# A step list of the sliding-window mixer reordered: unit 2's scores ahead of unit 1's value product, side steps up to two places later

## The chip, the cores and the metric

The kernel runs on one core of one Trainium2 chip. The metric is the time of one execution on the device in microseconds (us), lower is better. The engines are TensorE (PE in the rows, its weight loads PEld), VectorE (DVE), ScalarE (ACT), GpSimd (POOL) and SyncE (SP), which issues all the loads of weights.

## What is computed

Two models of two layers each run one after the other on a sequence of 256 positions with 1024 features. The change touches one sublayer only, the sliding-window attention with sinks in the last layer of the second model:

```python
def swa_sink_attention(h, wqkv, bqkv, qnorm, knorm, sinks, wo, bo):
    qkv = h @ wqkv + bqkv
    q, k, v = jnp.split(qkv, [ATTN_HEADS * HD, (ATTN_HEADS + KVH) * HD], axis=-1)
    q = rms_norm_2(q.reshape(bsz, T, KVH, G, HD), qnorm)
    k = rms_norm_2(k.reshape(bsz, T, KVH, HD), knorm)
    ...
    s = jnp.where(mask[None, :, None, None], s, -jnp.inf)      # scores, less a slope times distance
    p = jax.nn.softmax(jnp.concatenate([s, sink], axis=-1), axis=-1)[..., :-1]
    o = jnp.einsum('bnhgqk,bnkhd->bnqhgd', p.astype(h.dtype), vv)
    return o.reshape(bsz, T, ATTN_HEADS * HD) @ wo + bo
```

There are 16 query heads of 64 features and 4 heads of keys and values; the window is 128 positions. Ahead of this sublayer lie the whole first model and the second model's first layer and a feed-forward part; behind it a cross-attention to a memory (scores, softmax, value product, output projection) and a last feed-forward part.

## The kernel before, in words

Each engine has a program of its own, written out by hand, and the engines meet by semaphores only: an engine does its steps strictly in the order of its program and stops at the first one whose inputs are not there. Every dense product is made of three TensorE products of rounded halves (`hi` and `lo` of the weights, `thi` and `tlo` of the activations); ScalarE (L595) and VectorE (L607) split the weights that SyncE loads.

The sublayer is called `swa`. Its 16 heads and 256 positions are cut in six **units**, numbered 0 to 5. Units 0 to 2 have the first eight heads, units 3 to 5 the last eight. Units 0 and 3 are the first 128 positions with eight heads; the others are the last 128 positions with four heads and 256 keys. Each unit u has five **steps** (u, p):

- (u, 0) scores, on TensorE: two products that bring in the mask (L2869), then the score products (L2879), into banks 0 and 1 for an even unit and 2 and 3 for an odd one. With `lean` set it waits until unit u-2 has been copied out of the same banks.
- (u, 1) maxima, on VectorE: L996, L1006, L1010, L1011.
- (u, 2) exponentials, on ScalarE: L1066 for each head, L1069 for the sink.
- (u, 3) transposes of the probabilities: TensorE L963; VectorE sums the sink and inverts (L1018, L1021) and copies one half out (L1029); ScalarE copies the other half (L1073).
- (u, 4) value product: TensorE L978, and VectorE scales it into the output (L1047).

Beside these run **side steps**, one at each `None` of the list `SWA_PLAN`. They are written as generators on each engine, and the n-th `None` is the n-th piece of work of all of them. The ones that matter here:

- side step 4 (the last query quarter): TensorE makes the last quarter of the product with `wq2`, which gives the queries of heads 8 to 15 (six products, L645 to L647); VectorE takes both halves of the result out with the bias (L3008 twice; the second of them needs this quarter).
- side step 5 (squares and means): ScalarE squares these queries (L2962 twice), VectorE reduces and scales the sums (L3035, L3038 twice), and GpSimd raises them to a power (L841, twice).
- side step 6 (scaling): VectorE multiplies the queries by the result (L3045 twice).
- side step 7 (turning): TensorE transposes them (L728), ScalarE and VectorE write the rounded halves (L740, L757). Unit 3's scores need these.
- side step 8 transposes the outputs of units 0 to 2 (L728 again, ahead of unit 4's scores) and the following ones multiply them by the output weights (L645 to L647).

`placed` turns the list into the order of the unit steps and the places of the side steps, and `mixed` runs both in this order on TensorE, VectorE and ScalarE alike:

```python
    def mixed(main, side, places):
        at = 0
        for place in places:
            while at < place:
                next(main)
                at += 1
            next(side)
        run(side)
        run(main)
```

Of the kernel before, what the change touches and what calls it, by code (L numbers as in the profile page):

```python
# [456 lines left out]
def placed(plan):  # L457

    steps, places = [], []
    for x in plan:  # L460
        if x is None:
            places.append(len(steps))
        else:
            steps.append(x)
    return steps, places
# [32 lines left out]
class Kernel:  # L498
# [2360 lines left out]
    def swa_units(self):  # L2859
# [24 lines left out]
        for half in range(2):  # L2884
            for tt, h0, n in ((0, 8 * half, 8), (1, 8 * half, 4), (1, 8 * half + 4, 4)):
# [8 lines left out]

    SWA = {"k": (0, 4, 160), "q0": (512, 8, 96), "q1": (1024, 8, 0)}

    SWA_PLAN = [(0, 0), (0, 1), (1, 0), (0, 2), (1, 1), None, None, (0, 3), (1, 2), None, (0, 4), (1, 3), None, (1, 4),
# [3 lines left out]
    SWA_ORDER, SWA_BESIDE = placed(SWA_PLAN)  # L2901

# [847 lines left out]
```

How the kernel before makes its waits and increments, by code:

```python
def arms(e, c, flag, known, yes, no, stage):  # L378
    start, seen, chunks, splits = Counter(c.n), dict(c.seen), c.chunks, c.splits
    if c.dry:
        yes()
        after = Counter(c.n)
        c.n, c.chunks, c.splits = Counter(start), chunks, splits
        no()
        c.K.at["pad", stage, c.name] = Mark(c.name, max(after[c.name], c.n[c.name]))
        c.n[c.name] = c.K.at["pad", stage, c.name].value
    else:
        total = c.K.at["pad", stage, c.name].value
        for w in c.need(known):
            e.wait_ge(*w)
        seen = dict(c.seen)
        taken = e.value_load(flag, min_val=0, max_val=1)
        with e.If(taken == 1):
            yes()
            if c.n[c.name] < total:
                for w in c.need(c.last):
                    e.wait_ge(*w)
                e.nop().then_inc(*c.tick(by=total - c.n[c.name]))
        c.n, c.chunks, c.splits, c.seen = Counter(start), chunks, splits, dict(seen)
        with e.Else():
            no()
            if c.n[c.name] < total:
                for w in c.need(c.last):
                    e.wait_ge(*w)
                e.nop().then_inc(*c.tick(by=total - c.n[c.name]))
        c.seen = dict(seen)
    c.K.at["joined", stage, c.name] = c.last
# [167 lines left out]
    def load(self, s, c, i):  # L576
# [3 lines left out]
            if i >= NS:  # L580
                for w in c.need(("hi", i - NS, p), ("lo", i - NS, p)):
                    s.wait_ge(*w)
            b = (2 * i + p) % (2 * NS)
```

## Time and profile before

| what | value |
|---|---|
| time, median of 3 runs | 2207.06 us (2205.02 to 2209.64) |
| the profiled execution | 2209.44 us, span 2207.6 us |
| granted TensorE clock, mean of the span | 0.975 of full speed |
| TensorE matmuls busy | 95% of the span |
| VectorE, ScalarE, GpSimd busy | 70%, 56%, 2% |
| share of the 16 DMA engines used | 57.9% |

The span is what the trace covers; the profiled execution took 1.84 us more than it. The stretch that the change reorders lies between 1882 and 1908 us of the span. "Granted clock" is the share of TensorE's full clock of 2.4 GHz: 1.00 is 2.4 GHz and 0.50 is 1.2 GHz.

### The profile page before, as it was taken

The numbers are of one execution on the slowest core, as the hardware profiler recorded it, in microseconds if no ns is written. First come the engines' busy times: TensorE is split into PE (matmuls) and PEld (weight loads), VectorE is DVE, ScalarE is ACT, GpSimd is POOL, SyncE is SP. The second block draws the span as 40 slices with busy tenths as digits, with TensorE's granted clock in tenths as the row PEclk, the third lists the DMA queues.
The fourth block names the chain that finished last, engine by engine and source line by source line (L and its number), as shares of the span: only waits on it lengthen the run. The fifth ranks groups of instructions, "written<-read, shape, count | busy, mean of one in ns | idle before, by whom it ended". The sixth has DMA issues, their size and how long they took to land.

```text
span 2207.6 us, 32321 instructions
## 1 busy us (share of the span) xinstructions
PE 2095.2 (95%) x12148; PEld 1830.9 (83%) x12148; DVE 1545.2 (70%) x2158; ACT 1232.6 (56%) x1973; POOL 51.8 (2%) x64
## 2 busy tenths in 40 slices
PE   7988999989889999999999999999999999899999
PEld 5777888867677888878998987799999997779998
DVE  6568999986668999986555666566566566655655
ACT  4545777755546777755444564554444445454443
POOL 0000000000000000010000000000000001000000
PEclk9998999999989999999999999999999999899999
DMA  6233999973227999965556534255555555134553
GB/s 245 84 110 130 378 360 356 364 296 110 96 82 275 366 374 361 358 233 164 189 178 192 166 122 136 100 171 186 191 173 189 192 177 188 58 115 142 184 193 112
DMA packets 124214, 446.80 MB, mean 202 GB/s; under 512 B 14320, under 2 KB 15472, under 8 KB 123120
## 3 DMA queue, kind: packets, MB, share of 16 engines
q1 hardware_dynamic: 124048, 444.61, 57.9%
q8 instruction: 101, 1.65, 0.3%
q14 instruction: 65, 0.53, 0.1%
HBM read 443.51 MB, written 1.05 MB: 201 GB/s over the span
## 4 chain that ended last, share of the span: by engine, by line
PE 49%; DVE 3%; ACT 2%; issue 1%; DMA 0%; POOL 0%; DVEq 0%; SPq 0%; ACTq 0%
PE bank L686 8%; PE bank L688 8%; PE bank L687 8%; PE bank L1106 4%; PE bank L1105 4%; PE bank L1107 4%; PE bank L645 4%; PE bank L647 3%; PE bank L646 3%; PE bank L2725 1%; DVE lo L607 1%; PE bank L2707 1%; PE bank L978 1%; ACT hi L595 0%; DMA scr<-in_alibi 0%
## 5 line engine op out<-in xcount | busy, mean ns | idle before, releaser
L607 DVE TENSOR_TENSOR lo<-stage,hi 128x1024 fp32r<-128x1024 f32 (+1 forms) x834 | 971.6, 1207 | 233.5 <-ACT hi L595 206.6
L595 ACT ACTIVATE hi<-stage 128x1024 fp32r<-128x1024 f32 (+1 forms) x834 | 831.1, 1040 | 224.8 <-PE bank L647 83.6
L686 PE MATMUL bank<-thi,hi 128*128 128x256 f32 x1504 | 427.5, 284 | 5.1 <-DVE tlo L762 3.1
L687 PE MATMUL bank<-tlo,hi 128*128 128x256 f32 x1504 | 426.3, 283 | 0.0
L688 PE MATMUL bank<-thi,lo 128*128 128x256 f32 x1504 | 426.2, 283 | 0.0
L686 PEld LDWEIGHTS bank<-thi,hi 128*128 128x128 f32 x1504 | 289.2, 192 | 8.0 <-issue 6.5
L687 PEld LDWEIGHTS bank<-tlo,hi 128*128 128x128 f32 x1504 | 289.3, 192 | 1.4
L688 PEld LDWEIGHTS bank<-thi,lo 128*128 128x128 f32 x1504 | 289.2, 192 | 0.0
L645 PE MATMUL bank<-hi,thi 128*128 128x512 f32 (+3 forms) x648 | 253.9, 392 | 19.9 <-DVE tlo L762 6.9
L647 PE MATMUL bank<-hi,tlo 128*128 128x512 f32 (+3 forms) x648 | 248.0, 383 | 0.0
L646 PE MATMUL bank<-lo,thi 128*128 128x512 f32 (+3 forms) x648 | 247.9, 382 | 0.0
L2367 PE MATMUL bank<-hi,scr_r 128*128 128x512 f32 x512 | 206.5, 403 | 7.3 <-DVE scr_r L2497 5.8
L2369 PE MATMUL bank<-hi,scr_r 128*128 128x512 f32 x512 | 201.8, 394 | 0.0
L2368 PE MATMUL bank<-lo,scr_r 128*128 128x512 f32 x512 | 201.4, 393 | 0.0
L645 PEld LDWEIGHTS bank<-hi,thi 128*128 128x128 f32 x648 | 123.6, 191 | 47.1 <-issue 12.8
L647 PEld LDWEIGHTS bank<-hi,tlo 128*128 128x128 f32 x648 | 123.2, 190 | 23.4
L1131 ACT ACTIVATE scr<-scr 128x256 f32<-128x256 f32 x66 | 27.6, 418 | 204.2 <-DVE scr L1166 204.2
L646 PEld LDWEIGHTS bank<-lo,thi 128*128 128x128 f32 x648 | 123.6, 191 | 21.5 <-issue 0.4
L1105 PE MATMUL bank<-hi,ahi 128*128 128x512 f32 x352 | 137.5, 391 | 0.0
L1106 PE MATMUL bank<-lo,ahi 128*128 128x512 f32 x352 | 137.4, 390 | 0.0
L1107 PE MATMUL bank<-hi,alo 128*128 128x512 f32 x352 | 137.0, 389 | 0.0
L2367 PEld LDWEIGHTS bank<-hi,scr_r 128*128 128x128 f32 x512 | 97.1, 190 | 27.3 <-ACT hi L595 8.3
(395 smaller groups left out, 2709.8 us busy)
## 6 DMA issues: line engine op xcount, KB each, us to landing
stage<-in_exp SPq DMA_DIRECT2D x384, 512.0 KB, 5.3
stage<-in_ffn SPq DMA_DIRECT2D x264, 512.0 KB, 4.2
stage<-in_wi_a SPq DMA_DIRECT2D x16, 512.0 KB, 6.4
stage<-in_wi_b SPq DMA_DIRECT2D x16, 512.0 KB, 4.6
stage<-in_mem_wkv SPq DMA_DIRECT2D x16, 512.0 KB, 5.1
stage<-in_xwq SPq DMA_DIRECT2D x16, 512.0 KB, 4.2
stage<-in_xwo SPq DMA_DIRECT2D x16, 512.0 KB, 4.3
stage<-in_ssd_xbc SPq DMA_DIRECT2D x12, 512.0 KB, 3.8
```

The source lines that it names most:

```text
L595: a.activation(self.hi[i % NR][:, x:y], self.stage[(2 * i + p) % (2 * NS)][:, :y - x], ACT.Copy).then_inc(*c.tick(("hi", i, p), sem="hi"))
L607: v.tensor_tensor(self.lo[i % NR][:, x:y], self.stage[(2 * i + p) % (2 * NS)][:, :y - x], self.hi[i % NR][:, x:y].bitcast(F32), ALU.subtra ...
L645: t.matmul(out, thi[:, xs], hi[:, ws], start=(k0 + j == 0), stop=False)
L646: t.matmul(out, thi[:, xs], lo[:, ws], start=False, stop=False)
L647: m = t.matmul(out, tlo[:, xs], hi[:, ws], start=False, stop=(k0 + j == kt - 1))
L686: t.matmul(out, hi[:, ws], self.thi[:, xs], start=(k == 0), stop=False)
L687: t.matmul(out, hi[:, ws], self.tlo[:, xs], start=False, stop=False)
L688: m = t.matmul(out, lo[:, ws], self.thi[:, xs], start=False, stop=(k == 7))
L1105: t.matmul(out, self.ahi[:, xs], hi[:, ws], start=(f + j == 0), stop=False)
L1106: t.matmul(out, self.ahi[:, xs], lo[:, ws], start=False, stop=False)
L1107: m = t.matmul(out, self.alo[:, xs], hi[:, ws], start=False, stop=(f + j == nf - 1))
L2367: t.matmul(out, R["ghi"][:, xs], hi[:, ws], start=(k == 0), stop=False)
```

## The change

One table is edited: in `SWA_PLAN`, (2, 0) moves ahead of (1, 4), and of the side steps 4, 5, 6 and 7 each comes behind one or two unit steps that it stood ahead of. No instruction is added or removed, and the list has as many entries as before.

```diff
-    SWA_PLAN = [(0, 0), (0, 1), (1, 0), (0, 2), (1, 1), None, None, (0, 3), (1, 2), None, (0, 4), (1, 3), None, (1, 4),
-                (2, 0), None, (2, 1), None, (2, 2), (2, 3), None, (2, 4),
+    SWA_PLAN = [(0, 0), (0, 1), (1, 0), (0, 2), (1, 1), None, None, (0, 3), (1, 2), None, (0, 4), (1, 3), (2, 0), (1, 4),
+                None, (2, 1), (2, 2), None, (2, 3), None, (2, 4), None,
                 (3, 0), (3, 1), None, (4, 0), (3, 2), (4, 1), None, None, (3, 3), (4, 2), None, (3, 4), None,
```

**TensorE, from the transposes of unit 1 to the turning of the queries.** Before: L963 are transposes of probabilities, L645 to L647 the last query quarter, L978 a value product, L2869 and L2879 scores, L728 the turning.

```order
L963 MATMUL bank<-const_sb,scr 128x128 x8
L645 MATMUL bank<-hi,thi 128x512
...
L647 MATMUL bank<-hi,tlo 128x512
L978 MATMUL bank<-scr 128x64 x8
L2869 MATMUL bank<-scr_r,maskr 128x512 x2
L2879 MATMUL bank<-scr_r 128x256 x4
...
L963 MATMUL bank<-const_sb,scr 128x128 x8
L728 MATMUL bank<-const_sb,scr 128x128 x8
L978 MATMUL bank<-scr 128x64 x8
L2869 MATMUL bank<-scr_r,maskr 128x512 x2
```

After, the same place:

```order
L963 MATMUL bank<-const_sb,scr 128x128 x8
L2869 MATMUL bank<-scr_r,maskr 128x512 x2
L2879 MATMUL bank<-scr_r 128x256 x4
...
L978 MATMUL bank<-scr 128x64 x8
L645 MATMUL bank<-hi,thi 128x512
...
L647 MATMUL bank<-hi,tlo 128x512
L963 MATMUL bank<-const_sb,scr 128x128 x8
L978 MATMUL bank<-scr 128x64 x8
L728 MATMUL bank<-const_sb,scr 128x128 x8
L2869 MATMUL bank<-scr_r,maskr 128x512 x2
```

Unit 2's scores now stand ahead of unit 1's value product, the query quarter comes behind both, and the turning comes behind unit 2's value product instead of ahead of it.

**VectorE, the same stretch,** one piece of the difference. L3008 takes the queries out, L1047 scales a value product, L3035 and L3038 are the means, L996 to L1011 unit 2's maxima.

```order
 L1029 COPY scr<-bank 128x512
+L1047 TENSOR_TENSOR gb_<-bank,st 128x2x2x64
 L3008 SCALAR_TENSOR_TENSOR scr<-bank,st,rows 128x512 x2
-L1047 TENSOR_TENSOR gb_<-bank,st 128x2x2x64
+L996 TENSOR_REDUCE st<-bank 128x2 x2
+L1006 SCALAR_TENSOR_TENSOR st<-st,rows 128x4
+L1010 TENSOR_TENSOR st<-rows,st 128x4
+L1011 TENSOR_SCALAR st<-st 128x4
 L3035 TENSOR_REDUCE st<-scr 128x8
 L3038 TENSOR_SCALAR st<-st 128x8
```

The maxima of unit 2 now come ahead of the means but behind the taking out of the queries. Further down, the means stand ahead of unit 2's copy L1029, and the scaling L3045 behind it.

**ScalarE, from unit 1's copy on.** Before, the squares L2962 stand ahead of unit 2's exponentials L1066:

```order
L1073 ACTIVATE scr<-bank 128x512
L2962 ACTIVATE scr<-scr 128x512 x2
L1066 ACTIVATE scr,st<-bank,st 128x256 x4
L1069 ACTIVATE st<-st 128x4
L1073 ACTIVATE scr<-bank 128x512
```

After, they stand behind them:

```order
L1073 ACTIVATE scr<-bank 128x512
L1066 ACTIVATE scr,st<-bank,st 128x256 x4
L1069 ACTIVATE st<-st 128x4
L2962 ACTIVATE scr<-scr 128x512 x2
L1073 ACTIVATE scr<-bank 128x512
```

The squares moved behind the exponentials, and what follows from them moved with them. GpSimd's and SyncE's programs are the same as before.

## Rows read from the trace of the kernel before

**Rows 1.** The page: engine totals, and the chain that ended last.

```profile
PE 2095.2 (95%) x12148; PEld 1830.9 (83%) x12148; DVE 1545.2 (70%) x2158; ACT 1232.6 (56%) x1973; POOL 51.8 (2%) x64
...
PE 49%; DVE 3%; ACT 2%; issue 1%; DMA 0%; POOL 0%; DVEq 0%; SPq 0%; ACTq 0%
```

**Rows 2.** Windows: from:to, length, busy by engine, then granted clock, DMA share, GB/s.

```profile
1878.00:1888.00 10.00, 8.94 (x70) 7.58 (x68) 6.72 (x15) 4.00 (x13) 0.43 (x1) 1.00 0.32 107
...
1891.00:1908.00 17.00, 16.04 (x92) 14.60 (x92) 6.35 (x14) 5.94 (x22) 0.00 (x0) 0.50 0.00 0
1908.00:1918.00 10.00, 10.00 (x66) 8.16 (x64) 7.29 (x14) 5.35 (x19) 0.00 (x0) 1.00 0.35 107
```

**Rows 3.** Timeline, TensorE: start, length, instruction, count, idle time before it.

```profile
1882.06 1.04 PE L963 MATMUL bank<-const_sb,scr 128*128 128x128 f32 x8
...
1882.86 0.48 PE L645 MATMUL bank<-hi,thi 128*128 128x512 f32 x1
...
1884.33 1.89 PE L978 MATMUL bank<-scr 128*128 128x64 f32 x16
...
1886.04 0.72 PE L2869 MATMUL bank<-scr_r,maskr 128*128 128x512 f32 x2
...
1891.96 1.97 PE L963 MATMUL bank<-const_sb,scr 128*128 128x128 f32 x8 [4.07 <-ACT scr L1066]
...
1893.73 1.91 PE L728 MATMUL bank<-const_sb,scr 128*128 128x128 f32 x8
...
1895.43 3.52 PE L978 MATMUL bank<-scr 128*128 128x64 f32 x16
...
1898.71 1.20 PE L2869 MATMUL bank<-scr_r,maskr 128*128 128x512 f32 x2
...
1903.44 1.97 PE L728 MATMUL bank<-const_sb,gb_ 128*128 128x128 f32 x8
...
1908.17 0.50 PE L645 MATMUL bank<-hi,thi 128*128 128x512 f32 x1
```

**Rows 4.** Timeline, the other engines in the same stretch.

```profile
1882.26 0.69 DVE L1047 TENSOR_TENSOR gb_<-bank,st 128x512 f32<-128x512 f32 x1 [2.15 <-PE bank L978]
...
1883.75 1.53 DVE L3008 SCALAR_TENSOR_TENSOR scr<-bank,st,rows 128x512 f32<-128x512 f32 x2
...
1885.32 0.63 ACT L2962 ACTIVATE scr<-scr 128x512 f32<-128x512 f32 x1 [0.16 <-DVE scr L3008]
...
1887.39 0.68 DVE L3035 TENSOR_REDUCE st<-scr 128x8 f32<-128x512 f32 x1
...
1887.57 3.23 POOL L841 TENSOR_TENSOR st<-st,const_sb 128x8 f32<-128x8 f32 x2 [22.92 <-DVE st L3038]
...
1888.19 1.28 DVE L996 TENSOR_REDUCE st<-bank 128x2 f32<-128x512 f32 x2
...
1889.98 0.47 ACT L1066 ACTIVATE scr<-bank,st 128x256 f32<-128x256 f32 x1 [4.03 <-DVE st L1011]
...
1890.83 0.69 DVE L3045 TENSOR_TENSOR scr<-scr,st 128x512 f32<-128x512 f32 x1 [0.30 <-POOL st L841]
...
1891.79 0.21 ACT L1069 ACTIVATE st<-st 128x4 f32<-128x4 f32 x1
...
1893.97 0.69 DVE L1029 COPY scr<-bank 128x512 f32<-128x512 f32 x1 [1.56 <-PE bank L963]
...
1896.31 0.69 DVE L757 TENSOR_TENSOR scr_r<-bank,scr_r 128x512 fp32r<-128x512 f32 x1 [0.16 <-ACT scr_r L740]
```

**Rows 5.** Timeline, TensorE: the scores of unit 5, at the full clock.

```profile
1916.63 0.63 PE L2869 MATMUL bank<-scr_r,maskr 128*128 128x512 f32 x2
...
1918.33 1.09 PE L963 MATMUL bank<-const_sb,scr 128*128 128x128 f32 x8
```

**Rows 6.** Windows: the softmax of both cross-attentions of the second model.

```profile
1418.00:1424.00 6.00, 4.81 (x29) 4.39 (x28) 3.04 (x6) 2.27 (x8) 0.00 (x0) 0.72 0.00 0
...
1977.00:1987.00 10.00, 7.12 (x35) 6.32 (x34) 5.59 (x11) 4.34 (x14) 0.00 (x0) 0.66 0.01 2
```

## The prediction

> **What bounds the kernel now.** I read the page first. TensorE is busy 95% of the span and has 49% of the chain that ended last; no other engine has more than 3% of it [rows 1]. So an edit is worth what it does to TensorE's own stream: time in which TensorE waits, and the clock at which it works. Next I read the windows over the stretch that the list orders. Three stages are to be seen [rows 2]: up to 1888 TensorE works at the full clock; from 1891 to 1908 it is busy 16.04 of 17.00 us, but at a granted clock of 0.50; from 1908 on it is busy without a break at 1.00. Then the timeline. Ahead of unit 2's transposes at 1891.96 TensorE is idle for 4.07 us, waiting for ScalarE's exponentials [rows 3]. These began at 1889.98, when VectorE had the maxima ready, whose reduction began at 1888.19 [rows 4]. In front of that reduction VectorE's last piece of the means began at 1887.39 and took 0.68 us [rows 4]: VectorE, not TensorE, is late there. Behind the wait TensorE runs transposes, turning, value product, scores (1891.96, 1893.73, 1895.43, 1898.71) back to back [rows 3], at half the clock.
>
> So two things can be won or lost here: the idle time ahead of unit 2's transposes, and any new idle time on the way to unit 3's scores, which began at 1898.71.
>
> **The change, part by part.** All instructions stay. I replay the order with the durations of the rows; nothing moves before 1882.06.
>
> *Unit 2's scores earlier.* Unit 1's transposes take 0.80 us (1882.06 to 1882.86) [rows 3]. The scores need unit 0 out of their banks: VectorE's L1047 ends at 1882.26 + 0.69 = 1882.95 [rows 4]. They begin at about 1883.05 instead of 1886.04. At the full clock they take 1916.63 to 1918.33 = 1.70 us [rows 5], so they end at 1884.75. Unit 1's value product, 1.71 us (1884.33 to 1886.04) [rows 3], ends at 1886.46. The query quarter, 1.47 us (1882.86 to 1884.33) [rows 3], ends at about 1887.9, where TensorE was done before too. So far this is the same work in another order and costs nothing.
>
> *Unit 2's maxima.* By TensorE's account alone they could begin 3 us earlier. But on VectorE they now stand behind L3008 twice, and the second L3008 needs the query quarter, which now ends last. The pair took 1.53 us (0.75 each) [rows 4]. The quarter's result lands about 0.25 us behind its last issue (an estimate: it was issued until 1884.33, and the pair, begun at 1883.75, started its second half at about 1884.5 without a wait). So the second L3008 runs from 1888.15 to 1888.9, and the maxima begin at 1888.95 instead of 1888.19 [rows 4]: **0.76 us later**. What was taken off VectorE's path (the means, two times 0.68 and a short one each) is more than replaced by the wait for the quarter. The exponentials follow at the old distance (1889.98 - 1888.19 = 1.79), so at 1890.74, and the transposes at 1892.72. TensorE's idle time ahead of them grows from 4.07 to about 4.8 us.
>
> *Squares, means, power, scaling.* ScalarE now does both squares (0.63 us each [rows 4]) behind the exponentials, which end at 1891.79 + 0.21 + 0.76 = 1892.76. The squares end at 1893.45 and 1894.1. VectorE's means follow each (0.68 and a short operation of 0.17): done at 1894.4 and 1895.35. GpSimd needs 3.23 us for its two [rows 4]: 1894.5 to about 1897.75. Before, all this was hidden: it ran while TensorE waited for unit 2's exponentials anyway, and the second scaling began at 1890.83 [rows 4]. That cover is gone. Two things are now late:
>
> - unit 2's copy L1029 stands behind the means on VectorE. Sum, inverse (about 0.45 together) and the copy's 0.69 us [rows 4] end at 1896.55. Unit 2's value product waits for it and begins at 1896.65. The transposes end at 1894.7, so this is a **new wait of about 1.95 us** on TensorE;
> - the second scaling begins at 1897.8 and ends at 1898.5. At the slow clock that lies under the value product, which takes 3.3 us (1895.43 to 1898.71) [rows 3] and ends at 1899.95. Nothing is lost there.
>
> *Turning behind the value product.* Before, the turning's way through ScalarE and VectorE (1893.73 to 1896.31 + 0.69 = 1897.0, so 3.3 us) [rows 3, 4] lay beside the value product, and TensorE had no gap. Now nothing stands between the turning and unit 3's scores, which need its last half. From 1899.95 the turning takes TensorE about 1.8 us, and its results are there at 1903.3: a **second new wait of about 1.55 us**. Unit 3's scores begin at 1903.35 instead of 1898.71.
>
> Sum: 1903.35 - 1898.71 = **+4.64 us**. Made another way: 0.76 later transposes, 1.95 and 1.55 us of new waits, and about 0.4 for the latency of the transposes and the turning, which are no longer covered. Behind that point the order is the old one and TensorE goes on back to back; the chain behind it lies on TensorE, so the shift reaches the end whole. No load waits on it: in the slow stretch the DMA share is 0.00 [rows 2].
>
> *The clock.* Before, the granted clock fell to 0.50 during the idle stretch (it is 0.50 over 1891 to 1908) and stayed there although TensorE was busy 16.04 of 17.00 us, with transposes, a value product of 64 columns and score products of 64 rows [rows 2, 3]. It came back at 1908, with the mask and score products of unit 4, just ahead of dense products. In the changed kernel the idle time is longer, so I expect the fall too, and the same kinds of work behind it, now with two more gaps. So I take the return at the same place in the work. The bounds: a return at unit 3's scores saves half of what lies between 1898.71 and 1908.17, 9.46 / 2 = 4.7 us, at the most [rows 3]; a return only in the dense products behind 1908.17 costs an estimated 1 to 2.8 us (the twelve products there, at twice their 0.24 us each, as the six of a quarter take 1.47 us [rows 3]).
>
> The Trainium skill ("TensorE: Matmul & The Clock Gate", Part 1) says that an idle TensorE is put at 1.2 GHz, and that a busy one soon gets 2.4 GHz back. The fall agrees with rows 2; the return doesn't, since 16 busy microseconds did not bring it. By that rule the clock would be back early in unit 3's scores, the second rival below.
>
> **Rivals.**
>
> 1. *The stated one* (late maxima, two new waits, clock as before): +4.6 us, 2211.7. Chance 0.50.
> 2. *The clock comes back with unit 3's scores or the transposes behind them.* For it: TensorE would have been busy for some microseconds by then. Against it: 16.04 busy us at 0.50 [rows 2]. It gives back some 1 to 3 us: +1.6 to +3.6, 2208.7 to 2210.7. Chance 0.17.
> 3. *Slow for longer.* The two new gaps put off the return into the dense products, or the slow part in the softmax of the following cross-attention lasts longer. For it: that part has a clock of 0.66 over 10 us, and the like part one layer earlier 0.72 over 6 [rows 6], so 3.4 us lost against 1.7, with the same work: such parts move by about 1.7 us. +6 to +7.5, 2213 to 2214.5. Chance 0.18.
> 4. *Not slower: the clock doesn't fall, or is back before unit 2's value product.* The place is the idle stretch at 1888. The earlier scores shift TensorE's work in it, and if the clock stays at 1.00, then the value product ends at 1896.65 + 1.71 = 1898.4, the turning begins at 1898.6 when the scaling is done and is through in about 2.5 us (3.3 less the half of its 1.8 on TensorE), unit 3's scores begin at 1901.1, and the 9.46 us behind that become 4.7 to 5.3: 1905.8 to 1906.4 against 1908.17, so -2.4 to -1.8 us, 2205. It decides if the wait of 4.8 us stays under whatever makes the clock fall; 4.07 us did not [rows 3], so against it speaks every row there is. Chance 0.10.
> 5. *The change does what its order suggests:* unit 2's maxima gain from the earlier scores since VectorE gets past L3008 sooner than I reckon, and the copy slips in before the means are due. If the second L3008 ran 0.8 us sooner, the first 0.76 us are gone and the rest stays: +3.9. With both squares and power quicker still, nothing under +2.5: 2209.6 to 2211. Chance 0.05.
>
> **How the numbers follow.** The profiled execution took 2209.44 us, span 2207.6 and 1.84 around it; the median of the three runs is 2207.06. The sum of +4.6 against the profiled execution gives 2214.1, against the median 2211.7. I give the latter, since the profiled one was at the upper end of the runs. Its own range is 2210 to 2213.5. The whole range is 2207 to 2214.5: it leaves out rival 4 and a tail above rival 3. A measurement of this kernel can tell about 0.2% (4.4 us) from no change, so the forecast lies just above that bound, and the chances are near even. Slower by over 0.2%: somewhat more than half of case 1 (0.32) and all of case 3 (0.18), 0.50. Within 0.2%: the rest of case 1 (0.18), cases 2 and 5 (0.22), and most of case 4 (0.06), 0.46. Faster by over 0.2%: 0.04, where rival 4 also loses the slow part of the following cross-attention.
>
> **What the profile of the changed kernel would show.** L996 for unit 2 begins at about 1889 behind the second L3008, which itself waited for L647. TensorE idle 4.8 us ahead of L963 at 1892.7, about 1.9 us ahead of L978 (released by VectorE's L1029), about 1.5 us ahead of L2869 (released by L757). L2869 of unit 3 at about 1903.3. Clock 0.50 from 1891 until about 1911 to 1915. I am wrong if L978 does not wait for L1029, if the clock in 1893 to 1903 is 1.00, or if unit 3's scores begin before 1901.

## The result, and the profile after

The changed kernel takes 2213.7 us (median of 8 runs, 2211.28 to 2216.45), the kernel before, timed beside it, 2205.69 us. The ratio is 1.0033, interval 1.0023 to 1.0043: slower by 7.3 us, between 5 and 9.5 (the two medians differ by 8.0). The prediction was 2211.7 us in a range of 2207 to 2214.5, on a shift of +4.6. Four of the executions timed in the experiments took between 2519 and 7261 us and are left out of every ratio.

The page hardly moves; it is shown so that nobody looks there for 7 us.

```profile
PE 2095.8 (95%) x12148; PEld 1829.5 (83%) x12148; DVE 1546.2 (70%) x2158; ACT 1231.6 (56%) x1973; POOL 51.8 (2%) x64
```

TensorE's timeline in the changed kernel, against [rows 3]:

```profile
1880.38 1.05 PE L963 MATMUL bank<-const_sb,scr 128*128 128x128 f32 x8
...
1881.32 0.73 PE L2869 MATMUL bank<-scr_r,maskr 128*128 128x512 f32 x2
...
1884.94 0.48 PE L645 MATMUL bank<-hi,thi 128*128 128x512 f32 x1
...
1891.07 1.97 PE L963 MATMUL bank<-const_sb,scr 128*128 128x128 f32 x8 [4.48 <-ACT scr L1066]
...
1894.34 3.65 PE L978 MATMUL bank<-scr 128*128 128x64 f32 x16 [1.31 <-DVE scr L1029]
...
1897.78 1.91 PE L728 MATMUL bank<-const_sb,scr 128*128 128x128 f32 x8
...
1901.20 1.19 PE L2869 MATMUL bank<-scr_r,maskr 128*128 128x512 f32 x2 [1.50 <-DVE scr_r L757]
...
1910.11 0.50 PE L645 MATMUL bank<-hi,thi 128*128 128x512 f32 x1
```

And the other engines, against [rows 4]:

```profile
1887.29 1.28 DVE L996 TENSOR_REDUCE st<-bank 128x2 f32<-128x512 f32 x2
...
1889.08 0.47 ACT L1066 ACTIVATE scr<-bank,st 128x256 f32<-128x256 f32 x1 [7.46 <-DVE st L1011]
...
1890.98 1.16 ACT L2962 ACTIVATE scr<-scr 128x512 f32<-128x512 f32 x2
...
1891.66 0.69 DVE L3035 TENSOR_REDUCE st<-scr 128x8 f32<-128x512 f32 x1 [2.62 <-ACT scr L2962]
...
1892.63 3.23 POOL L841 TENSOR_TENSOR st<-st,const_sb 128x8 f32<-128x8 f32 x2 [30.05 <-DVE st L3038]
...
1893.54 0.66 DVE L1029 COPY scr<-bank 128x512 f32<-128x512 f32 x1
...
1895.90 0.69 DVE L3045 TENSOR_TENSOR scr<-scr,st 128x512 f32<-128x512 f32 x1 [0.91 <-POOL st L841]
```

The starts must be read from a common point, since executions reach this stretch at different times. Over all fourteen traces read here unit 1's transposes begin between 1876.07 and 1888.40 us, though the programs ahead of them are the same: 12 us of spread that has nothing to do with the change. Counted from unit 1's transposes, unit 2's begin at 10.69 us (before 9.90) and unit 3's scores at 20.82 (before 16.65). Both new waits are there, each with the releaser that was named, 1.31 us by the copy L1029 and 1.50 us by L757.

Windows of the changed kernel: the clock is at half (1.2 GHz) for 20.5 us.

```profile
1880.38:1888.80 8.42, 6.20 (x50) 4.94 (x49) 4.73 (x11) 0.60 (x1) 0.00 (x0) 1.00 0.05 19
1888.80:1909.30 20.50, 15.42 (x82) 13.27 (x84) 8.86 (x21) 6.83 (x21) 3.23 (x2) 0.50 0.00 0
1909.30:1914.00 4.70, 4.70 (x35) 4.02 (x34) 3.22 (x7) 4.42 (x16) 0.00 (x0) 1.00 0.00 0
```

From here on "the stretch" is the time from the start of unit 1's transposes to the first product of the output weights (L645 behind unit 4's scores). In the two traces it is 1908.17 - 1882.06 = 26.11 us before and 1910.11 - 1880.38 = 29.73 after: +3.62 us, half of what the medians say.

### The profile page after: what moved, and what is told of

It is laid out like the page before. It is cut to its first block, busy times and chain, and to the rows that moved or that the text cites. A ratio compares the mean times of both kernels' runs of the same rounds, so it can differ in the third digit from the quotient of the medians.

```text
span 2209.4 us, 32321 instructions
## 1 busy us (share of the span) xinstructions
PE 2095.8 (95%) x12148; PEld 1829.5 (83%) x12148; DVE 1546.2 (70%) x2158; ACT 1231.6 (56%) x1973; POOL 51.8 (2%) x64
## 4 chain that ended last, share of the span: by engine, by line
PE 49%; DVE 3%; ACT 2%; issue 1%; DMA 0%; POOL 0%; DVEq 0%; SPq 0%; ACTq 0%
PE bank L686 8%; PE bank L687 8%; PE bank L688 8%; PE bank L1106 4%; PE bank L1105 4%; PE bank L1107 4%; PE bank L645 4%; PE bank L647 3%; PE bank L646 3%; DVE lo L607 1%; PE bank L2725 1%; PE bank L2707 1%; PE bank L978 1%; PE bank L2879 0%; DMA scr<-in_alibi 0%
## 5 line engine op out<-in xcount | busy, mean ns | idle before, releaser
L645 PE MATMUL bank<-hi,thi 128*128 128x512 f32 (+3 forms) x648 | 255.8, 395 | 19.9 <-DVE tlo L762 6.9
L647 PE MATMUL bank<-hi,tlo 128*128 128x512 f32 (+3 forms) x648 | 249.5, 385 | 0.0
L645 PEld LDWEIGHTS bank<-hi,thi 128*128 128x128 f32 x648 | 124.7, 192 | 47.5 <-issue 12.6
L647 PEld LDWEIGHTS bank<-hi,tlo 128*128 128x128 f32 x648 | 124.3, 192 | 23.8
```

The lines of the kernel that those rows point to most:

```text
L645: t.matmul(out, thi[:, xs], hi[:, ws], start=(k0 + j == 0), stop=False)
L647: m = t.matmul(out, tlo[:, xs], hi[:, ws], start=False, stop=(k0 + j == kt - 1))
```

## The experiments

All ratios are to the kernel before, timed beside each experiment on the same chip. `e1` to `e8` ran on one chip; `e9` to `e12` ran on another, where the median of the kernel before was 2207.54 us against 2205.83 and 2206.21, so kernels from the two groups are compared by their ratios and not by their times.

**One part each.** `e1_norm_steps` keeps quarter and scores where they were:

```diff
-    ... (0, 4), (1, 3), None, (1, 4), (2, 0), None, (2, 1), None, (2, 2), (2, 3), None, (2, 4),
+    ... (0, 4), (1, 3), None, (1, 4), (2, 0), (2, 1), (2, 2), None, (2, 3), None, (2, 4), None,
```

> This is the kernel before with one part of the change: the squares and means, the scaling and the turning (side steps 5, 6, 7) follow the steps of unit 2 as in the changed kernel; the query quarter and unit 2's scores stay where they were before. Theory A (two new waits are the main cost: the value product of unit 2 waits for the copy that now stands behind the means, and unit 3's scores wait for the turning): unit 2's transposes begin 0.2 us earlier than before relative to unit 1's transposes, since the maxima wait for the scores alone, and unit 3's scores 3.6 us later than before. In all +3.5 to +6 us over before. Rival B (the late maxima and the longer idle time ahead of unit 2's transposes are the main cost): without them the time is that of before within 1.5 us.

Measured 2212.62 us, ratio 1.0029 (1.0018 to 1.0039), nearly all of the change. Its TensorE rows:

```profile
1878.35 1.04 PE L963 MATMUL bank<-const_sb,scr 128*128 128x128 f32 x8
...
1887.99 1.97 PE L963 MATMUL bank<-const_sb,scr 128*128 128x128 f32 x8 [3.83 <-ACT scr L1066]
...
1891.27 3.65 PE L978 MATMUL bank<-scr 128*128 128x64 f32 x16 [1.31 <-DVE scr L1029]
...
1898.13 1.19 PE L2869 MATMUL bank<-scr_r,maskr 128*128 128x512 f32 x2 [1.50 <-DVE scr_r L757]
```

Unit 2's transposes begin at 9.64 us, 0.26 earlier than before, and the idle time ahead of them is shorter. The two waits are those of the changed kernel to the hundredth. Rival B, that the late maxima are the main cost, has fallen. The size was at the upper edge of what was expected: the ratio gives +6.4 us, expected were +3.5 to +6, although unit 3's scores were only 3.13 us later than before (expected 3.6). The stretch is 29.06 us, and the clock was at half for 20.5 us of it.

`e2_scores_quarter` has the other part:

```diff
-    ... (0, 4), (1, 3), None, (1, 4), (2, 0), None, (2, 1), None, (2, 2), (2, 3), None, (2, 4),
+    ... (0, 4), (1, 3), (2, 0), (1, 4), None, None, (2, 1), None, (2, 2), (2, 3), None, (2, 4),
```

> This is the kernel before with the other part of the change: unit 2's scores and the query quarter are moved as in the changed kernel, and the norm steps (squares and means, scaling, turning) stand where they stood before, so the means stay ahead of unit 2's maxima. Theory A: VectorE's second taking out of the queries waits for the quarter until about 6.1 us after the start of unit 1's transposes, the means follow, and unit 2's maxima begin 2.3 us later than before; the two waits of the norm steps are absent. Unit 3's scores 2.3 us later than before, in all +2 to +4 us. Rival B (the late maxima are the main cost of the changed kernel): as slow as the changed kernel or slower, +7 us. Rival C (scores first are a gain by themselves): faster than before.

Measured 2209.4 us, ratio 1.0008 (0.9997 to 1.0018). That is +1.8 us (-0.7 to +4.0), expected were +2 to +4. Rival B is out: it is not as slow as the changed kernel. Rival C, a gain, is not seen, and anything above 0.7 us is excluded.

```profile
1882.30 0.75 DVE L3008 SCALAR_TENSOR_TENSOR scr<-bank,st,rows 128x512 f32<-128x512 f32 x1 [0.36 <-PE bank L647]
...
1884.55 1.28 DVE L996 TENSOR_REDUCE st<-bank 128x2 f32<-128x512 f32 x2
...
1888.32 1.97 PE L963 MATMUL bank<-const_sb,scr 128*128 128x128 f32 x8 [6.07 <-ACT scr L1066]
```

The second L3008 waits for the quarter (L647), and unit 2's transposes begin 12.25 us behind unit 1's at 1876.07, 2.35 late as expected. TensorE idles for 6.07 us, more than in any other order. Yet the stretch took 23.12 us in this trace, less than the 26.11 of the kernel before: the clock was at half for only 6.9 us. This did not fit my picture of a slow part that belongs to the order, and led to the repeats below.

**The clock: fill the idle time.** `e3_fill_before` and `e4_fill_after` add products that nobody reads, 16 to the kernel before and 18 to the changed one (the lines below them move by two):

```diff
             elif p == 3:
+                for _ in range(16 if S == "swa" and u == 2 else 0):
+                    t.matmul(self.bank[3][:, :], self.identr, self.thi[:, 0:512], start=True, stop=True)
```

> The kernel before, with 16 products of 128x512 of the rounded identity with the activations into a bank that nobody reads (bank 3), put ahead of unit 2's transposes on TensorE. They take about 3.7 us at the full clock and lie in the 4.07 us in which TensorE waits there. They are additional work and leave the result as it is. Theory A (the idle time makes the granted clock fall, and the slow stretch behind it costs 7 us): the clock stays 1.00 from 1891 to 1908, unit 2's transposes begin where they did, unit 3's scores 3 us earlier, and the whole is 6 to 8 us faster than before. Rival B (the clock falls because of what kinds of products run there, not because of the idle time): the clock is 0.50 there as before, and the time is the same or 1 us slower.

Measured 2203.76 us, ratio 0.9983 (0.9972 to 0.9994). The mechanism is as expected, with the clock at 1.00 through both halves of the stretch, 19.39 us long:

```profile
1881.77:1891.66 9.89, 9.77 (x66) 7.93 (x65) 7.78 (x18) 3.84 (x12) 3.24 (x2) 1.00 0.08 30
1891.66:1901.16 9.50, 9.03 (x92) 7.84 (x93) 5.74 (x14) 4.07 (x13) 0.00 (x0) 1.00 0.00 1
```

The same transposes, turning, value product and scores ran at the full clock once the idle time ahead of them was filled. So the fall hangs on the idle time and not on the kinds of products alone, and rival B is out. But against the first trace 6.7 us are saved, and the ratio gives 3.7 (1.3 to 6.2). The expected 6 to 8 us in the median were wrong: the usual run of the kernel before does not lose that much.

> The changed kernel with 18 such products (about 4.1 us at the full clock) ahead of unit 2's transposes, in its wait of 4.5 us. Theory A: with the full clock kept, value product, turning and scores of units 3 and 4 run at the full clock, 6 to 7 us faster than the changed kernel; the wait for the copy grows to about 2.4 us, since the transposes take half the time, and that ahead of unit 3's scores stays at 1.5 us. If that wait of 2.4 us makes the clock fall again, only 1 to 3 us are gained. Compared with the kernel before with filling it is 2.5 to 4.5 us slower: this is what the order costs without the clock. Rival B (clock falls regardless): the time of the changed kernel.

Measured 2215.3 us, ratio 1.0035 (1.0021 to 1.0049): nothing gained over the changed kernel.

```profile
1887.96 4.38 PE L958 MATMUL bank<-thi,maskr 128*128 128x512 f32 x18
...
1895.88 2.07 PE L980 MATMUL bank<-scr 128*128 128x64 f32 x16 [2.19 <-DVE scr L1031]
...
1901.71 1.19 PE L2871 MATMUL bank<-scr_r,maskr 128*128 128x512 f32 x2 [1.50 <-DVE scr_r L757]
```

```profile
1881.93:1897.60 15.67, 13.22 (x92) 10.95 (x91) 8.26 (x21) 4.15 (x13) 3.23 (x2) 1.00 0.05 21
1897.60:1911.30 13.70, 11.88 (x72) 9.71 (x70) 5.32 (x11) 4.64 (x18) 0.00 (x0) 0.50 0.00 1
```

With the first wait filled, the second one grew to 2.19 us (expected 2.4). The clock fell at 1897.6, inside the value product that follows this wait, and stayed at half for 13.7 us. So the new wait for the copy can be followed by the fall too; the one ahead of unit 3's scores came when the clock was at half already, and no run shows what it does alone. Expected were 1 to 3 us of gain in this case; the stretch is 1911.20 - 1881.93 = 29.27 us, 0.6 less than the 29.87 of the changed kernel (three traces, below), and the median gained nothing.

**Repeats of both kernels,** one trace each.

> The kernel before once more, for a second trace. The trace shown of before took 3.6 us more than the median of its runs. Theory A (how long the slow clock lasts behind the idle time differs from run to run in the kernel before, and is long in each run of the changed kernel): the clock falls again ahead of unit 2's transposes, and comes back either by 1898 (then from unit 1's transposes to the first product of the output weights it takes 20 to 24 us and the run is near 2203 us) or at 1905 to 1909 as in the first trace (26 us, 2207 to 2210 us). Rival B (it is a fixed property of this order): 17 us slow and 26.1 us from transposes to product again, whatever the run's time.

> A third trace of the kernel before. Theory A: slow for 3 to 7 us behind unit 2's transposes (22 to 24 us from unit 1's transposes to the first product of the output weights, like the second trace's 22.4), or, less often, for 17 us (26 us). In no case the 29.7 to 30.0 us of the changed kernel.

> The changed kernel once more, for a second trace. Theory A: the two new waits (1.3 us ahead of unit 2's value product, 1.5 us ahead of unit 3's scores) are there again to 0.1 us and the slow clock lasts from the idle stretch until unit 4's scores or later, so 29 to 31 us from unit 1's transposes to the first product of the output weights. Rival B (the clock comes back early in some runs of the changed kernel too): 24 to 27 us.

> A third trace of the changed kernel. Theory A: 29 to 31 us from unit 1's transposes to the first product of the output weights, with the slow clock for 17 to 21 us. A value of 27 us or less would say that the clock comes back early in some of its runs too.

The second trace of the kernel before (the run took 2205.69 us), and behind it the third (2202.98 us):

```profile
1890.00:1896.90 6.90, 4.79 (x23) 4.79 (x24) 3.54 (x9) 3.82 (x12) 0.95 (x1) 0.51 0.00 0
1896.90:1903.65 6.75, 6.29 (x71) 5.30 (x71) 3.67 (x10) 2.34 (x9) 0.00 (x0) 1.00 0.00 1
```

```profile
1888.80:1892.20 3.40, 2.80 (x13) 2.80 (x14) 1.20 (x4) 1.24 (x6) 0.00 (x0) 0.50 0.00 0
1892.20:1900.07 7.87, 7.39 (x82) 6.41 (x80) 4.71 (x11) 3.43 (x11) 0.00 (x0) 1.00 0.00 1
```

One thing in the second trace does not belong to the wait of 4.07 us. The clock had already been at half from 1879.8 to 1883.2, and unit 1's transposes, with which the stretch begins, took 1.91 us instead of 1.04:

```profile
1881.28 1.91 PE L963 MATMUL bank<-const_sb,scr 128*128 128x128 f32 x8
```

Unit 2's transposes therefore begin at 10.83 us in it and not at 9.90, so 0.93 of its 22.37 us come from this earlier slow part. The 6.9 us in the table below leave it out.

The second (2219.75 us) and third (2213.95 us) of the changed kernel:

```profile
1897.50:1918.00 20.50, 16.11 (x88) 13.96 (x90) 8.62 (x19) 7.09 (x25) 3.23 (x2) 0.50 0.00 0
```

```profile
1891.70:1912.20 20.50, 15.79 (x84) 13.63 (x86) 8.62 (x19) 7.09 (x23) 3.23 (x2) 0.50 0.00 0
```

| kernel | the stretch, us | at half clock from the wait ahead of unit 2's transposes on, us |
|---|---|---|
| before, three traces | 26.11, 22.37, 20.57 | 17.1, 6.9, 3.4 |
| changed, three traces | 29.73, 30.02, 29.85 | 20.5, 20.5, 20.5 |

The same order, with the same wait of 4.07 us in all three traces, had its slow part end in unit 4's scores once, in unit 2's value product once, and in the turning once. Rival B of the repeats, a fixed property of the order, is out for the kernel before. In the changed kernel all three agree. The means, 23.0 and 29.9, differ by 6.8 us. From unit 1's transposes to the end of the span it is 325.54, 322.32 and 321.60 us before and 329.02, 329.30 and 329.18 after, 6.0 us more in the mean. Both lie in the 5 to 9.5 us that the ratio gives.

Three traces for each kernel are few, but the other orders point the same way. Where new waits of this kind stood open (`e1`, `e4`, and `e7` below) the half clock lasted 20.5, 13.7 and 17.1 us; where none did (`e2`, and `e8` below) 6.9 and 3.4. In all that is 13.7 us or more in six of six traces with new waits, and more than 6.9 in one of five without. That the waits keep the clock down is what these counts suggest; no run changed them alone with all else in its place and time.

**All three waits filled.** `e9_fill_all_after` puts 9 such products ahead of the value product of unit 2 and 6 ahead of unit 3's scores, besides the 18:

```diff
             if p == 0:
+                for _ in range(6 if S == "swa" and u == 3 else 0):
+                    t.matmul(self.bank[3][:, :], self.identr, self.thi[:, 0:512], start=True, stop=True)
...
             elif p == 4:
+                for _ in range(9 if S == "swa" and u == 2 else 0):
+                    t.matmul(self.bank[3][:, :], self.identr, self.thi[:, 0:512], start=True, stop=True)
```

> The changed kernel with products nobody reads (as in the filled kernels before) in all three of its waits: 18 ahead of unit 2's transposes, 9 ahead of its value product, 6 ahead of unit 3's scores. Theory A (the waits cut TensorE's work up and so keep the clock at half until unit 4; this is the larger part of what the change costs): the clock stays full through the stretch; from unit 1's transposes to the first product of the output weights 24 to 25.5 us instead of 29.7 and 30.0 in the two traces of the changed kernel, 4 to 6 us faster in the median. What is left against the filled kernel before (19.4 us) is 5 us, the waits themselves. Rival B (the clock falls in spite of the filling): 29 us, and the time of the changed kernel or 1 us more.

Measured 2209.61 us, ratio 1.0010 (1.0000 to 1.0020), against 1.0033 without filling: about 5 us gained by additional work.

```profile
1882.84:1893.50 10.66, 10.40 (x68) 8.32 (x67) 4.97 (x12) 2.58 (x11) 0.00 (x0) 1.00 0.08 30
1893.50:1907.64 14.14, 12.90 (x108) 10.52 (x108) 8.53 (x20) 5.00 (x15) 3.23 (x2) 1.00 0.01 2
```

The stretch is 24.80 us, all of it at the full clock. With the filled kernel before this splits the cost. The order alone costs 24.80 - 19.39 = 5.4 us at the full clock, all of it by unit 3's scores (19.06 us behind unit 1's transposes against 13.64). The ratios of the two filled kernels, 1.0010 and 0.9983, say 6.0 us. The clock costs the kernel before 23.0 - 19.4 = 3.6 us on average and the changed one 29.9 - 24.8 = 5.1. So of the 6.8 us, 5.4 are the order (later transposes and waits) and 1.4 are clock. The 5.4 rests on one trace of each filled kernel, and the 1.4 also on the mean of three unlike traces of the kernel before, so its size is rough.

**Two other orders.** `e7_maxima_then_norm`:

```diff
-    ... (0, 4), (1, 3), (2, 0), (1, 4), None, (2, 1), (2, 2), None, (2, 3), None, (2, 4), None,
+    ... (0, 4), (1, 3), None, (2, 0), (2, 1), (1, 4), None, (2, 2), (2, 3), None, (2, 4), None,
```

> A new order from what the runs showed: the query quarter stays first, unit 2's scores and its maxima both come ahead of unit 1's value product, the means behind them, the scaling behind unit 2's copy, the turning behind its value product as in the changed kernel. Theory: VectorE is not held by the quarter, unit 2's transposes begin 8.0 us behind unit 1's (before 9.9), TensorE's wait ahead of them is 2.4 us instead of 4.1. If the clock stays full, unit 3's scores begin 14.2 us behind unit 1's transposes (before 16.65) and the kernel is 3 to 7 us faster than before. If it falls, the wait for the turning costs more than was won: +1 us over before.

Measured 2210.79 us, ratio 1.0030 (1.0018 to 1.0041). Unit 2's transposes begin at 7.87 us and wait for 1.90, but the copy and the turning are waited for again (0.87 and 1.50 us), and the clock fell all the same and stayed at half for 17.1 us, from 0.6 us behind the start of these transposes on:

```profile
1891.00 1.49 PE L963 MATMUL bank<-const_sb,scr 128*128 128x128 f32 x8 [1.90 <-ACT scr L1066]
```

The stretch is 26.11 us, as long as in the first trace of before. That I priced this case at +1 us and not at +3 or more was the same mistake as in the prediction: that trace was taken for the usual run. Against the mean of the three traces of before the stretch is 3.1 us longer, while the ratio gives +6.6 (4.0 to 9.0): its one trace does not account for the rest.

`e8_maxima_means_kept` leaves all norm steps ahead and moves only unit 1's value product:

```diff
-    ... (0, 4), (1, 3), None, (1, 4), (2, 0), None, (2, 1), None, (2, 2), (2, 3), None, (2, 4),
+    ... (0, 4), (1, 3), None, (2, 0), None, (2, 1), (1, 4), (2, 2), None, (2, 3), None, (2, 4),
```

> As the kernel before, but unit 1's value product moved behind unit 2's scores and maxima on TensorE, VectorE and ScalarE; quarter, means, scaling and turning keep their order and stay ahead. VectorE does not wait for that product before the means and the maxima. Theory: unit 2's transposes begin 8.7 us behind unit 1's (before 9.9), the wait ahead of them is 3.0 us, none of the two new waits of the changed kernel appears, and unit 3's scores begin 12.2 us behind if the clock is full, 15.5 us if it is half (before 16.65 at half). So 1 to 8 us faster than before in the stretch, 1 to 5 us in the median. Rival (the clock decides alone, and it falls as before): within 1 us of before.

Measured 2204.11 us, ratio 0.9992 (0.9982 to 1.0003): not to be told from no change. Transposes at 8.49 us behind a wait of 2.53, and 3.4 us at half clock; the stretch is 19.31 us in its one trace, but how long the usual run is slow was not traced. Last, the same with 10 products in the wait:

> The order in which unit 1's value product stands behind unit 2's maxima and the norm steps are left where they were, and 10 products nobody reads ahead of unit 2's transposes, in the wait of 2.5 us. Theory A: no fall of the clock behind the wait; from unit 1's transposes to the first product of the output weights 18.0 us (the same order without filling 19.3, with 3.4 us at half clock; the kernel before with filling 19.4): 1 to 2 us faster than the kernel before with filling, 3 to 5 us faster than before. Rival B: the clock is full there in most runs without filling too, and nothing is gained over the order alone (0.1% under before).

Measured 2203.7 us, ratio 0.9979 (0.9968 to 0.9991), the best of all, with the stretch as expected:

```profile
1880.14:1888.64 8.50, 8.37 (x61) 6.82 (x60) 7.70 (x18) 3.84 (x12) 3.23 (x2) 1.00 0.10 39
1888.64:1898.13 9.49, 9.02 (x93) 7.84 (x93) 5.75 (x14) 4.07 (x13) 0.00 (x0) 1.00 0.00 1
```

The stretch is 17.99 us, 1.4 less than in `e3_fill_before`. Its ratio cannot be told from that kernel's 0.9983, so that the order adds to the filling is seen in the traces alone.

## Why the prediction was right, and where its sizes were off

- *The number, 2211.7 in 2207 to 2214.5:* measured 2213.7, and that it lies inside is in part luck. The upper end allows a shift of +7.4 over the 2207.06 us of that time. The kernel before measured 2205.69 this time, so the shift is 7.3 us by the ratio and 8.0 by the medians. The 2213.7 is also just above the 2210 to 2213.5 that the stated case had for itself. Reckoned against the profiled execution the same sum gave 2214.1, which is nearer, since that execution had the long slow part that the changed kernel has in every trace.
- *Unit 2's scores earlier is worth nothing:* right. They began at 0.94 us behind unit 1's transposes, predicted 0.99.
- *Maxima 0.76 us later:* measured 0.79 at unit 2's transposes. `e2` shows the cause by itself (L3008 released by L647) and its price is small in the time, 0.08%.
- *New wait for the copy, 1.95 us:* the place and releaser are right, the size is 1.31. I had taken each squares row at its full 0.63 us and each means row with a gap; back to back the two squares take 1.16 and VectorE lost nothing between its short operations. The copy ended 3.13 us behind the start of unit 2's transposes, reckoned 3.83.
- *New wait ahead of unit 3's scores, 1.55 us:* measured 1.50.
- *Sum at unit 3's scores, +4.64:* measured +4.17 between the first two traces, short by the copy's term (0.64 us) and over by 0.2 in what the latencies add.
- *The shift reaches the end whole:* from the end of the stretch to the end of the span it is 299.43 us before and 299.29 after in the first traces, so yes. In the two quicker traces of before it is 299.95 and 301.03: there 0.5 and 1.6 us of what the full clock wins are lost again behind the stretch. A wait of 0.95 us ahead of the next value product, which the first trace does not have, is part of it; what the rest is stays open.
- *The clock returns "at the same place in the work":* this is the step that failed. Against the first trace of before it was nearly right (half clock 17.1 and 20.5 us). But that slow part was not a property of the kernel before: the other two traces had 6.9 and 3.4 us. In these the clock returns early, and TensorE has its work behind the wait in one piece; the changed order has two waits in this place, and stayed slow in three of three traces, each time until unit 4's scores. So for the changed kernel the return was where I put it, and what was wrong is the base: the long slow part was charged to both kernels alike, while the kernel before has it only in some runs. The shift is therefore larger than the sum, 7.3 against 4.6 us.
- *Rival 3* (slow for longer) has the price that was measured (+6 to +7.5), but not by its mechanism: the return was not put off into the dense products, and the cross-attention is not what differs, since what lies behind the stretch takes 299.3 us in all three traces of the changed kernel, not more than before. Its 3.4 us lost there is a bound and not a loss, too: TensorE was busy for only 7.12 of those 10 us [rows 6]. *Rival 2*, an early return, occurred in two of three traces of the kernel before and in none of the changed one. *Rivals 4 and 5* did not occur.
- The Trainium skill's rule ("TensorE: Matmul & The Clock Gate", Part 1), that a busy TensorE soon gets 2.4 GHz back, agrees with the second and third traces of before and not with the first, where 16.04 busy us of 17 went by at half clock [rows 2]. Its statement that idle time brings the clock down agrees with all six traces of the two kernels, where it fell within the wait ahead of unit 2's transposes, and with the three kernels whose waits in the stretch were all filled, where it stayed up. How much idle time it takes no run here settles: in `e4` and `e7` it fell behind waits of 2.19 and 1.90 us, with TensorE at work again.

## What to carry to other kernels

A chain of small steps on other engines (squares, means, power, scaling, turning) cost nothing here as long as it ran under a wait that was there anyway. Put behind that wait, it was paid for wherever the matrix engine had nothing else to do, and more at the full clock (unit 3's scores 5.4 us later) than at half (4.17): the chain takes as long as before, and the matrix engine's own work beside it takes half the time. Before a scores step is moved forward, look at what stands in front of its reader on the other engine: here the maxima waited for a product that the move had pushed back. And one trace of a kernel whose clock falls is one draw: take two or three of both kernels before pricing a slow part, and compare starts from a common event, not from the span's start.

## What was not expected of the hardware

- How long the half clock lasts after the same idle time of 4.07 us and the same instructions differs from run to run: 17.1, 6.9 and 3.4 us. What decides it stays open; the moment within the run at which the wait falls is a candidate, and no run here varied it alone.
- Work that nobody reads made the kernel faster: 16 products of 128x512 in the wait gave 0.17% (0.06 to 0.28), and 33 in three waits took 5 us off the changed kernel. Filling only the longest of three waits gave nothing.
- The clock fell behind shorter waits too: in `e7` 0.6 us into the transposes that follow a wait of 1.90 us, and in `e4` 1.7 us into the value product that follows one of 2.19 us. In the changed kernel it fell earlier, 2.3 us before the wait of 4.48 us ended (1888.8 against 1891.07).
